# Per-layer embedding by halves of a tile, and token tiles behind both of them

## The chip, the cores and the metric

The kernel runs on one core of a Trainium2 chip. The metric is the device time of one execution in microseconds (us). All arithmetic is float32. Weight products run in the type float32r: each operand is split into a high and a low part, and three matmuls (weights low by input high, high by high, high by low) make one product.

## The reference

256 tokens of width 1024 pass through two layers of one kind and one of another. `PLAN` in the kernel lists the ten stages: ffn, even, ffn, ple, ffn, mla, ffn, ple, hybrid, ffn. The stages that matter here are:

```python
def rms_norm(x, g):
    y = x * lax.rsqrt(jnp.mean(x * x, axis=-1, keepdims=True) + EPS)
    return y * g

def swiglu(h, w_gate, w_up, w_down):
    return (jax.nn.silu(h @ w_gate) * (h @ w_up)) @ w_down

def per_layer_embedding(h, p_i, w_gate, w_proj, post_norm):
    return rms_norm(jax.nn.sigmoid(h @ w_gate) * (p_i @ w_proj), post_norm)

x = x + per_layer_embedding(rms_norm(x, g[3]), p[i], ple_w_gate[i], ple_w_proj[i], g[4])
# after the first one: x = x + 0.5 * swiglu(rms_norm(x, g[0]), ...)
# after the second one, the hybrid layer:
h = rmsnorm(x, norm_mix)
u = h @ w_in          # split into q, k, v, z, xbc (896 wide), dt_raw, p_in
y = concatenate([moba_attention(q, k, v), ssd_mixer(conv(xbc), z, dt_raw), pool_mixer(p_in)])
x = x + y @ w_out
```

`ple_w_gate` is 1024 x 1024, `ple_w_proj` 256 x 1024.

## The kernel before

**Weights.** Every weight is streamed in slots of 128 x 2048 floats (1 MB). Three raw slots form a ring (`raw`), filled by SyncE's DMAs in the order of use; `load_slot` waits until the low half of the slot three places earlier has been made (`split_ready`). ScalarE copies a raw slot into its high half (`wh`, `split_high`, L211), once the matmuls that used that place have run (`weights_used`); VectorE makes the low half (`wl`, `split_low`, L222); TensorE waits for it in `take_slot`. Slots are numbered through the program; `act_ahead.through(n)` and `dve_ahead.through(n)` issue all splits up to slot n at that place of the engine's instruction stream. So each engine's program order fixes where its splits stand among the rest.

**Columns.** The input of a product is x turned: TensorE transposes x in 128 x 128 blocks into PSUM, ScalarE scales them with the norm's gain into `hth` (high), VectorE makes `htl` (low). `turn_x`, `turn_act` and `turn_dve` do this for both token tiles (tt = 0, 1) of a pair of feature blocks k. `turn_tile`, `tile_act` and `tile_dve` (L375, L381, L388) do it for four blocks of one token tile. The row factor of the norm is applied after the product; it is the power of a mean of squares, made by GpSimd (`norm_pool`, L428 and L429).

**PLE** (`ple_pe`, `ple_act`, `ple_dve`, `ple_pool`). With n its first slot: n is the proj weight, n+1 to n+4 are the gate weight, and the next stage begins with n+5 and n+6. TensorE multiplies proj into PSUM banks 0 to 3 and then the gate into banks 4 to 7; the last two gate slots are taken tile by tile. Then, a tile at a time: sigmoid of 1024 columns (L853, ScalarE), product with the proj result (L889, VectorE), squares (L858, ScalarE) and times the gain (L894, VectorE), power (L879, GpSimd), and two additions of 512 columns into x (L901, VectorE). Each addition releases transposes of TensorE (`x_ready`).

**Behind it.** The FFN (`first_by_tiles`) takes its first two slots tile by tile: four feature blocks of tile 0 with slot n+5, four with n+6, and tile 1's transposes stand behind the sixth. The hybrid instead waits for all of x: 44 transposes of the identity fill the time (L837), sixteen transposes of x follow, and `columns_product` multiplies slots n+5 and n+6 with the weights stationary and 256 tokens moving. VectorE takes the result of these two slots (`xa`, L2338, 1024 columns) times the row factor, and later that of the next two (`xb`).

Of the kernel before, what the change touches and what calls it, by code (L numbers as in the profile page):

```python
# [31 lines left out]
def build_block(nc, io, out):  # L32
# [4 lines left out]
    P = 128  # L37
# [39 lines left out]
    with ExitStack() as stack:  # L77
# [5 lines left out]

        raw = sb("raw", [P, RING, SLOT])
# [33 lines left out]
        lb = sb("lb", [P, 3, 4])  # L118
        arena = sb("arena", [P, 20552])
# [28 lines left out]
        cols_low = sem("cols_low")  # L148
        silu_ready = sem("silu_ready")
# [45 lines left out]

        def first_part(t, n, j):

            return t[:, n, j * SLOT // 2:(j + 1) * SLOT // 2]

        def split_high(act, n):  # L200
# [8 lines left out]
            if n >= RING:  # L209
                act.wait_ge(weights_used, n - RING + 1)  # L210
            nc.scalar.activation(wh[:, n % RING, 0:width[n]], raw[:, n % RING, 0:width[n]], ACT.Copy)\  # L211
              .then_inc(high_ready, 1)

        def split_low(dve, n):
            if n < 2:
                for j, (ready, done) in enumerate(((first_high, first_low), (high_ready, split_ready))):
# [5 lines left out]
            nc.vector.tensor_tensor(wl[:, n % RING, 0:width[n]], raw[:, n % RING, 0:width[n]],  # L222
                                    wh[:, n % RING, 0:width[n]].bitcast(f32), ALU.subtract)\
# [146 lines left out]

        def turn_tile(pe, s, tt, u):

            pe.wait_ge(x_ready, 4 * (s - 1) + 2 * tt + u + 1)
            for k in range(4 * u, 4 * u + 4):
                m = nc.tensor.transpose(ps[:, 4 + 2 * tt + u, (k % 4) * P:(k % 4 + 1) * P], x[:, tt, k * P:(k + 1) * P], ident[:, :])  # L375
            m.then_inc(turned, 1)

        def tile_act(act, s, tt, u, gain):
            act.wait_ge(turned, bank_base[s][0] + 2 * tt + u + 1)
            for k in range(4 * u, 4 * u + 4):  # L380
                m = nc.scalar.activation(hth[:, k, tt * P:(tt + 1) * P], ps[:, 4 + 2 * tt + u, (k % 4) * P:(k % 4 + 1) * P], ACT.Copy,  # L381
                                         scale=cols[:, gain + k:gain + k + 1])
            m.then_inc(cols_high, 1)

        def tile_dve(dve, s, tt, u, gain):
            dve.wait_ge(cols_high, bank_base[s][0] + 2 * tt + u + 1)
            for k in range(4 * u, 4 * u + 4):
                m = nc.vector.scalar_tensor_tensor(out=htl[:, k, tt * P:(tt + 1) * P], in0=ps[:, 4 + 2 * tt + u, (k % 4) * P:(k % 4 + 1) * P],  # L388
                                                   scalar=cols[:, gain + k:gain + k + 1], in1=hth[:, k, tt * P:(tt + 1) * P].bitcast(f32),
                                                   op0=ALU.mult, op1=ALU.subtract)  # L390
            m.then_inc(cols_low, 1)

# [123 lines left out]
        def ffn_pe(pe, n, s, f):  # L516
# [51 lines left out]
            def first_by_tiles(pe):  # L568

                turn_tile(pe, s, 0, 0)  # L570
                turn_tile(pe, s, 0, 1)
                for tt in range(TT):
                    for u in range(2):
                        take_slot(pe, n + u)
                        turned_by(pe, s, 0, 2 * tt + u + 1)
                        r = (n + u) % RING
                        for kk in range(4):
                            k, at = 4 * u + kk, kk * 2 * HC
                            m = product(bank(tt), hth[:, k, tt * P:(tt + 1) * P], htl[:, k, tt * P:(tt + 1) * P],
                                        wh[:, r, at:at + 2 * HC], wl[:, r, at:at + 2 * HC], k == 0, k == KT - 1)  # L580
# [167 lines left out]
        def after_ple(s):  # L748
            return s > 0 and PLAN[s - 1:s + 1] == ["ple", "ffn"]
# [14 lines left out]
        ple_gate = Steps(sem("ple_act"), ["sigmoid0", "squares0", "sigmoid1", "squares1"], 2)  # L764
        ple_vector = Steps(sem("ple_dve"), ["product0", "gained0", "product1", "gained1"], 2)
# [6 lines left out]
        ple_ms = arena[:, 4096:4096 + TT]  # L772
# [19 lines left out]
        def ple_pe(pe, s, l):  # L792
# [31 lines left out]
            for tt in range(TT):  # L824
                for j in (2, 3):
                    take_slot(pe, n + 1 + j)
                    for kk in range(2):
                        for half in range(2):
# [1901 lines left out]
```

## Time and profile before

| | us |
|---|---|
| median of 3 runs (1378.53 to 1378.92) | 1378.87 |
| the profiled execution | 1378.48 |
| its span in the trace | 1376.7 |
| TensorE busy in the span | 1341.6 |
| VectorE busy | 796.8 |
| ScalarE busy | 645.7 |
| GpSimd busy | 82.2 |

The mean granted clock of TensorE was 0.996 of full. Matmuls are pipelined: a matmul of 512 columns stands with 0.39 us in the trace, while the next starts 0.227 us after it.

### The profile page before, as it was taken

Reading aid. Unit: us, or ns where it says so; the run is one execution under the profiler, and the core shown is the slowest. Engines: PE = TensorE matmul, PEld = TensorE weight load, DVE = VectorE, ACT = ScalarE, POOL = GpSimd, SP = SyncE. Lnnn points to the kernel's source line nnn. Section 1 sums busy time; section 2 is a strip of 40 time slices with the busy share of each in tenths; the row PEclk is TensorE's granted clock in tenths of the full one; section 3 lists DMA queues with packets and bytes.
Section 4 is the critical chain, followed back from the end, with each engine's and each line's share of the span. In section 5 each row is a group of like instructions: output and inputs, shape, how many; then the busy total and the mean of one; then the engine's idle time right before and its main releaser. Section 6 shows DMA issues by size and latency. Waiting matters only on the chain.

```text
span 1376.7 us, 17712 instructions
## 1 busy us (share of the span) xinstructions
PE 1341.6 (97%) x6710; PEld 1114.1 (81%) x6710; DVE 796.8 (58%) x873; ACT 645.7 (47%) x742; POOL 82.2 (6%) x181
## 2 busy tenths in 40 slices
PE   8999999999999999999999999999999998999998
PEld 7888889877888887788888877888887986788886
DVE  5555459746545545654556876544556887555444
ACT  5444457324444445544444856444445655444442
POOL 2000003100000001200000300000001200000000
PEclk9999999999999999999999999999999999999999
DMA  8655555414655554455553514655543452565551
GB/s 256 218 190 183 183 168 184 153 62 150 219 190 194 186 183 153 155 190 191 192 188 113 193 61 160 201 185 191 191 164 138 156 184 63 175 204 183 183 191 54
DMA packets 159326, 233.32 MB, mean 169 GB/s; under 512 B 7608, under 2 KB 126542, under 8 KB 159278
## 3 DMA queue, kind: packets, MB, share of 16 engines
q1 hardware_dynamic: 156560, 229.17, 50.5%
q10 hardware_dynamic: 2238, 2.70, 0.6%
q0 software_dynamic: 480, 0.80, 0.4%
q8 instruction: 32, 0.52, 0.2%
q14 instruction: 16, 0.13, 0.0%
HBM read 231.58 MB, written 1.05 MB: 169 GB/s over the span
## 4 chain that ended last, share of the span: by engine, by line
PE 92%; DVE 4%; ACT 2%; issue 1%; DMA 0%; POOL 0%; ACTq 0%; DVEq 0%; POOLq 0%
PE ps L250 27%; PE ps L252 26%; PE ps L251 26%; PE ps L545 2%; DVE wl L222 1%; PE ps L1012 1%; PE ps L266 1%; PE ps L334 1%; PE ps L268 1%; PE ps L267 1%; DVE htl L367 1%; PE ps L1526 1%; PE ps L1525 1%; ACT wh L211 1%; ACT hth L354 0%
## 5 line engine op out<-in xcount | busy, mean ns | idle before, releaser
L250 PE MATMUL ps<-wl,hth 128*128 128x512 f32 (+2 forms) x1280 | 504.6, 394 | 14.5 <-DVE htl L367 5.8
L252 PE MATMUL ps<-wh,htl 128*128 128x512 f32 (+2 forms) x1280 | 494.7, 386 | 0.0
L251 PE MATMUL ps<-wh,hth 128*128 128x512 f32 (+2 forms) x1280 | 493.9, 386 | 0.0
L714 DVE TENSOR_TENSOR wl<-raw,wh 128x2048 fp32r<-128x2048 f32 x120 | 275.1, 2292 | 204.9 <-ACT wh L663 204.9
L250 PEld LDWEIGHTS ps<-wl,hth 128*128 128x128 f32 x1280 | 240.5, 188 | 65.0 <-issue 15.2
L663 ACT ACTIVATE wh<-raw 128x2048 fp32r<-128x2048 f32 x120 | 229.7, 1914 | 123.6 <-PE ps L252 123.6
L252 PEld LDWEIGHTS ps<-wh,htl 128*128 128x128 f32 x1280 | 240.3, 188 | 49.3
L251 PEld LDWEIGHTS ps<-wh,hth 128*128 128x128 f32 x1280 | 240.8, 188 | 44.6
L222 DVE TENSOR_TENSOR wl<-raw,wh 128x2048 fp32r<-128x2048 f32 (+3 forms) x98 | 217.1, 2223 | 79.5 <-ACT wh L211 79.3
L211 ACT ACTIVATE wh<-raw 128x2048 fp32r<-128x2048 f32 (+3 forms) x98 | 181.0, 1853 | 65.7 <-PE ps L252 45.5
L250 PE MATMUL ps<-wl,prod_h 128*128 128x512 f32 x400 | 156.1, 390 | 0.0
L252 PE MATMUL ps<-wh,prod_l 128*128 128x512 f32 x400 | 155.8, 390 | 0.0
L251 PE MATMUL ps<-wh,prod_h 128*128 128x512 f32 x400 | 155.6, 389 | 0.0
L650 ACT ACTIVATE silu_g<-ps,rstd 128x256 f32<-128x256 f32 x110 | 46.3, 472 | 173.2 <-PE ps L252 173.2
L655 ACT ACTIVATE prod_h<-ps 128x512 fp32r<-128x512 f32 x50 | 29.9, 599 | 156.3 <-PE ps L545 156.3
L700 DVE SCALAR_TENSOR_TENSOR prod<-ps,rstd,silu_g 128x256 f32<-128x256 f32 x110 | 48.2, 479 | 83.7 <-ACT silu_g L650 83.7
L252 PEld LDWEIGHTS ps<-wh,prod_l 128*128 128x128 f32 x400 | 75.1, 188 | 15.6
L251 PEld LDWEIGHTS ps<-wh,prod_h 128*128 128x128 f32 x400 | 75.1, 188 | 15.4
L250 PEld LDWEIGHTS ps<-wl,prod_h 128*128 128x128 f32 x400 | 75.1, 188 | 15.4
L707 DVE TENSOR_TENSOR prod_l<-ps,prod_h 128x512 fp32r<-128x512 f32 x50 | 34.6, 692 | 71.7 <-ACT prod_h L655 71.7
L428 POOL TENSOR_SCALAR mean_sq<-mean_sq 128x1 f32<-128x1 f32 x20 | 8.4, 420 | 864.6 <-ACT xn L415 860.9
L354 ACT ACTIVATE hth<-ps,cols 128x256 fp32r<-128x256 f32 x77 | 30.3, 478 | 49.6 <-PE ps L334 44.4
(377 smaller groups left out, 990.7 us busy)
## 6 DMA issues: line engine op xcount, KB each, us to landing
raw<-in_ffn_w_down SPq DMA_DIRECT2D x88, 512.0 KB, 4.0
raw<-in_ffn_w_gate SPq DMA_DIRECT2D x86, 512.0 KB, 4.0
raw<-in_ffn_w_up SPq DMA_DIRECT2D x86, 512.0 KB, 4.9
raw<-in_w_gate_up SPq DMA_DIRECT2D x44, 512.0 KB, 4.7
raw<-in_even_w_in SPq DMA_DIRECT2D x24, 512.0 KB, 4.6
raw<-in_w_down SPq DMA_DIRECT2D x22, 512.0 KB, 3.6
raw<-in_ple_w_gate SPq DMA_DIRECT2D x16, 512.0 KB, 4.1
raw<-in_w_in SPq DMA_DIRECT2D x16, 512.0 KB, 4.4
```

Source lines behind the costliest of these rows:

```text
L211: nc.scalar.activation(wh[:, n % RING, 0:width[n]], raw[:, n % RING, 0:width[n]], ACT.Copy)\
L222: nc.vector.tensor_tensor(wl[:, n % RING, 0:width[n]], raw[:, n % RING, 0:width[n]], wh[:, n % RING, 0:width[n]].bitcast(f32), ALU.subtract)\
L250: nc.tensor.matmul(o, xh, b, start=first, stop=False)
L251: nc.tensor.matmul(o, xh, a, start=False, stop=False)
L252: return nc.tensor.matmul(o, xl, a, start=False, stop=last)
L354: m = nc.scalar.activation(dst[:, k, :], ps[:, banks[b], o:o + T], ACT.Copy, scale=g)
L650: nc.scalar.activation(silu_g[:, tt, :], ps[:, b + tt, 0:HC], ACT.Silu, scale=rstd[:, tt:tt + 1]).then_inc(silu_ready, 1)
L655: nc.scalar.activation(to[:, :, :], bank(b).rearrange("p (k t) -> p k t", k=2), ACT.Copy)\
L663: nc.scalar.activation(wh[:, r, :], raw[:, r, :], ACT.Copy).then_inc(high_ready, 1)
L700: m = nc.vector.scalar_tensor_tensor(out=prod[:, tt, :], in0=ps[:, b + tt, HC:2 * HC], scalar=rstd[:, tt:tt + 1], in1=silu_g[:, tt, :], op ...
L707: nc.vector.tensor_tensor(to[:, :, :], bank(b).rearrange("p (k t) -> p k t", k=2), high[:, :, :].bitcast(f32), ALU.subtract).then_inc(prod ...
L714: nc.vector.tensor_tensor(wl[:, r, :], raw[:, r, :], wh[:, r, :].bitcast(f32), ALU.subtract)\
```

## The change

- Two spare pairs of weight halves, `spare_h` and `spare_l`, lie over a part of the arena that PLE and the start of the next stage don't use. The two slots behind each PLE (n+5, n+6) are split into them; ScalarE's split of these waits for the raw data and for no matmul. ScalarE and VectorE issue the splits through n+6 ahead of the sigmoids.
- VectorE splits slot n+1 between the first and the second pair of column banks.
- Sigmoid, product, squares and gain are done in halves of 512 columns; GpSimd adds the two sums of squares.
- The last gate slot's pieces are sorted by half, and TensorE's first four transposes of x (tile 0) stand ahead of the last gate piece of tile 1. Tile 1's transposes stand behind the whole of tile 0's products.
- The columns of a tile are handed on first as a pair of blocks (`pair_high`, `pair_low`), then the rest of the four; they lie in other PSUM banks.
- The hybrid, too, begins by tiles: its first two slots are multiplied for 128 tokens at a time, with one PSUM bank for each tile and slot, so VectorE adds the slots' results up. The 44 filler transposes are gone.

```diff
+        SPARE = 10240
+        with ExitStack() as lower:
+            lower.enter_context(nc.sbuf_tensor("below_spare", [P, SPARE], f32))
+            spare_h = lower.enter_context(nc.sbuf_tensor("spare_h", [P, 2, SLOT], f32r))
+            spare_l = lower.enter_context(nc.sbuf_tensor("spare_l", [P, 2, SLOT], f32r))
         arena = sb("arena", [P, 20552])
+        spare = {base[s] + u: u for s in range(1, len(PLAN)) if PLAN[s - 1] == "ple" for u in range(2)}
...
-            if n >= RING:
+            if n >= RING and n not in spare:
                 act.wait_ge(weights_used, n - RING + 1)
-            nc.scalar.activation(wh[:, n % RING, 0:width[n]], raw[:, n % RING, 0:width[n]], ACT.Copy)\
+            nc.scalar.activation(high_of(n)[:, 0:width[n]], raw[:, n % RING, 0:width[n]], ACT.Copy)\
...
+        def tile_bank(tt, u, i):
+            return 4 + 2 * tt + i if u == 0 else (1, 5)[tt]
+        def tile_by(pe, s, tt, k):
+            if k == 0:
+                pe.wait_ge(pair_low, TT * ples[s - 1] + tt + 1)
+            if k in (2, 4):
+                turned_by(pe, s, 0, 2 * tt + k // 4 + 1)
...
             def first_by_tiles(pe):
-                turn_tile(pe, s, 0, 0)
-                turn_tile(pe, s, 0, 1)
                 for tt in range(TT):
                     for u in range(2):
                         take_slot(pe, n + u)
-                        turned_by(pe, s, 0, 2 * tt + u + 1)
                         for kk in range(4):
                             k, at = 4 * u + kk, kk * 2 * HC
+                            tile_by(pe, s, tt, k)
...
-                            if tt == 0 and k == 5:
-                                turn_tile(pe, s, 1, 0)
-                                turn_tile(pe, s, 1, 1)
+                    if tt == 0:
+                        turn_tile(pe, s, 1, 0)
+                        turn_tile(pe, s, 1, 1)
...
         def ple_pe(pe, s, l):
+                    pieces = [(kk, half) for kk in range(2) for half in range(2)]
+                    if j == 3:
+                        pieces.sort(key=lambda v: v[1])
+                    for i, (kk, half) in enumerate(pieces):
+                        if tt == 1 and j == 3 and i == 3:
+                            turn_tile(pe, s + 1, 0, 0)
+                        m = gate_piece(j, kk, half, tt)
+                        if j == 3 and (i == 1 or (i == 3 and tt == 0)):
+                            m.then_inc(tile_ready, 1)
...
-            for _ in range(0 if after_ple(s + 1) else 44):
-                nc.tensor.transpose(ps[:, 4, 0:P], ident[:, :], ident[:, :])
+            turn_tile(pe, s + 1, 0, 1)
         def ple_act(act, s, l):
-            act_ahead.through(act, n + 5)
+            act_ahead.through(act, n + 6)
...
+            sigmoid(0, 0)
+            sigmoid(0, 1)
+            squares(0, 0)
+            squares(0, 1)
+            sigmoid(1, 0)
+            tile_act(act, s + 1, 0, 0, gain_behind(s + 1))
+            sigmoid(1, 1)
+            tile_act(act, s + 1, 0, 1, gain_behind(s + 1))
+            squares(1, 0)
+            squares(1, 1)
+            act.wait_ge(ple_vector.sem, ple_vector.after("gained11", l))
+            nc.scalar.activation(xn[:, 0, :], x[:, 0, :], ACT.Square, scale=1 / math.sqrt(D),
+                                 accum_out=mean_sq[:, 0:1]).then_inc(sq_ready, 1)
+            act_ahead.through(act, n + 7)
         def ple_dve(dve, s, l):
-            turn_dve(dve, s, 1, KT, GAINS + (5 * l + 3) * KT, PLE_BANKS)
-            dve_ahead.through(dve, n + 5)
+            turn_dve(dve, s, 1, KT, GAINS + (5 * l + 3) * KT, PLE_BANKS, part=(0, 2))
+            dve_ahead.through(dve, n + 1)
+            turn_dve(dve, s, 1, KT, GAINS + (5 * l + 3) * KT, PLE_BANKS, part=(2, 4))
+            dve_ahead.through(dve, n + 6)
...
+            gated(0, 0)
+            gated(0, 1)
             gain(0)
             add(0)
+            gated(1, 0)
+            tile_dve(dve, s + 1, 0, 0, gain_behind(s + 1))
+            gated(1, 1)
+            tile_dve(dve, s + 1, 0, 1, gain_behind(s + 1))
             gain(1)
             add(1)
...
+        PART_BANK = ((0, 4), (2, 3))
         def hybrid_pe(pe, s):
-            for b in range(4):
-                turn_x(pe, s, b, b)
-            columns_product(pe, n, [bank(4 + j, T) for j in range(4)], 512, first_of=s)
+            for tt in range(TT):
+                for u in range(2):
+                    take_slot(pe, n + u)
+                    for j in range(4):
+                        for kk in range(4):
+                            k = 4 * u + kk
+                            if j == 0:
+                                tile_by(pe, s, tt, k)
+                            o, c = ps[:, PART_BANK[tt][u], j * P:(j + 1) * P], kk * 512 + j * P
+                            a, b = high_of(n + u)[:, c:c + P], low_of(n + u)[:, c:c + P]
+                            nc.tensor.matmul(o, b, hth[:, k, tt * P:(tt + 1) * P], start=kk == 0, stop=False)
+                            nc.tensor.matmul(o, a, hth[:, k, tt * P:(tt + 1) * P], start=False, stop=False)
+                            m = nc.tensor.matmul(o, a, htl[:, k, tt * P:(tt + 1) * P], start=False, stop=kk == 3)
...
+                if tt == 0:
+                    turn_tile(pe, s, 1, 0)
+                    turn_tile(pe, s, 1, 1)
...
         def hybrid_dve(dve, s):
-            HY_DVE.done(nc.vector.tensor_tensor(h_x[:, 0:4, PADC:PADC + T], ps[:, 4:8, 0:T], repeated(r_row[:, :], 1, 4), ALU.mult), "xa")
+            parts = [h_x[:, 0:4, PADC + tt * P:PADC + (tt + 1) * P] for tt in range(TT)]
+            for tt in range(TT):
+                a, b = (bank(PART_BANK[tt][u]).rearrange("p (j c) -> p j c", j=4) for u in range(2))
+                r = repeated(r_row[:, tt * P:(tt + 1) * P], 1, 4)
+                nc.vector.tensor_tensor(parts[tt], a, r, ALU.mult)
+                m = nc.vector.tensor_tensor(h_c[:, 0:4, tt * P:(tt + 1) * P], b, r, ALU.mult)
+            dve_link(dve, m)
+            for tt in range(TT):
+                m = nc.vector.tensor_tensor(parts[tt], parts[tt], h_c[:, 0:4, tt * P:(tt + 1) * P], ALU.add)
+            HY_DVE.done(m, "xa")
```

`norm_tiles_act` and `tile_dve` take the place of `norm_act` and `norm_dve` at the hybrid's start, and the p product's results lie in banks 2 and 3 in place of 4 and 5.

## Rows read from the trace of the kernel before

**Rows 1.** The page: busy time by engine, and the chain that ended last by engine.

```profile
PE 1341.6 (97%) x6710; PEld 1114.1 (81%) x6710; DVE 796.8 (58%) x873; ACT 645.7 (47%) x742; POOL 82.2 (6%) x181
...
PE 92%; DVE 4%; ACT 2%; issue 1%; DMA 0%; POOL 0%; ACTq 0%; DVEq 0%; POOLq 0%
```

**Rows 2.** Timeline of PE (start, duration, instruction, idle before): first gate matmul.

```profile
526.06 0.47 PE L250 MATMUL ps<-wl,hth 128*128 128x512 f32 x1 [1.71 <-DVE wl L222]
```

**Rows 3.** Timeline of DVE, start of the first PLE.

```profile
518.44 1.66 DVE L367 SCALAR_TENSOR_TENSOR htl<-ps,cols,hth 128x256 fp32r<-128x256 f32 x4
522.06 1.66 DVE L367 SCALAR_TENSOR_TENSOR htl<-ps,cols,hth 128x256 fp32r<-128x256 f32 x4 [1.96 <-ACT hth L354]
523.64 4.48 DVE L222 TENSOR_TENSOR wl<-raw,wh 128x2048 fp32r<-128x2048 f32 x2
```

**Rows 4.** Timeline of POOL, the two powers of the norm.

```profile
526.09 2.46 POOL L429 TENSOR_TENSOR rstd<-mean_sq,minus_half 128x1 f32<-128x1 f32 x1
...
528.93 0.57 POOL L429 TENSOR_TENSOR rstd<-mean_sq,minus_half 128x1 f32<-128x1 f32 x1
```

**Rows 5.** Timeline of ACT, first PLE.

```profile
522.63 1.94 ACT L211 ACTIVATE wh<-raw 128x2048 fp32r<-128x2048 f32 x1
...
529.53 1.92 ACT L211 ACTIVATE wh<-raw 128x2048 fp32r<-128x2048 f32 x1 [2.89 <-POOL rstd L429]
...
539.26 1.28 ACT L853 ACT_TABLE_LOAD   x1
542.71 1.12 ACT L853 ACTIVATE xn<-ps,rstd 128x1024 f32<-128x1024 f32 x1 [2.16 <-PE ps L252]
...
548.97 2.18 ACT L381 ACTIVATE hth<-ps,cols 128x128 fp32r<-128x128 f32 x8 [0.83 <-PE ps L375]
```

**Rows 6.** Line L179, 534.1 to 535 us: slot n+6's two loads until landed.

```profile
DMA to landing us min/median/max: 4.0/4.5/5.0
```

**Rows 7.** Timeline of DVE, end of the first PLE.

```profile
547.41 1.42 DVE L901 SCALAR_TENSOR_TENSOR x_rows<-arena,x_rows 128x512 f32<-128x512 f32 x2 [1.00 <-POOL arena L879]
550.15 2.16 DVE L388 SCALAR_TENSOR_TENSOR htl<-ps,cols,hth 128x128 fp32r<-128x128 f32 x8 [1.33 <-ACT hth L381]
```

**Rows 8.** Timeline of PE, first PLE to the FFN's third slot.

```profile
548.30 1.23 PE L375 MATMUL ps<-ident,x_rows 128*128 128x128 f32 x8 [0.19 <-DVE x_rows L901]
551.42 0.47 PE L250 MATMUL ps<-wl,hth 128*128 128x512 f32 x1 [1.88 <-DVE htl L388]
...
561.18 0.48 PE L250 MATMUL ps<-wl,hth 128*128 128x512 f32 x1 [0.44 <-DVE htl L388]
...
566.72 0.39 PE L250 MATMUL ps<-wl,hth 128*128 128x512 f32 x1
```

**Rows 9.** Timeline of PE, second PLE and the hybrid's start.

```profile
1060.49 4.96 PE L837 MATMUL ps<-ident 128*128 128x128 f32 x44
...
1068.64 0.36 PE L266 MATMUL ps<-hth,wl 128*128 128x256 f32 x1 [0.62 <-DVE htl L367]
...
1080.21 0.61 PE L458 MATMUL ps<-silu_g,ones 128*128 128x128 f32 x4
...
1100.60 0.60 PE L2024 MATMUL ps<-ident,arena 128*128 128x128 f32 x4
```

**Rows 10.** Timeline of PE elsewhere: narrow matmuls in the even and the mla stage.

```profile
272.69 2.26 PE L1048 MATMUL ps<-arena 64*128 64x128 f32 x24
...
754.94 0.27 PE L250 MATMUL ps<-wl,hth 128*128 128x192 f32 x1
...
757.17 0.27 PE L252 MATMUL ps<-wh,htl 128*128 128x192 f32 x1
```

**Rows 11.** Timeline of DVE, start of the hybrid.

```profile
1081.32 1.22 DVE L2338 TENSOR_TENSOR arena<-ps,r_row 128x1024 f32<-128x1024 f32 x1
...
1089.42 1.24 DVE L222 TENSOR_TENSOR wl<-raw,wh 128x1048 fp32r<-128x1048 f32 x1
...
1098.35 2.28 DVE L222 TENSOR_TENSOR wl<-raw,wh 128x2048 fp32r<-128x2048 f32 x1
```

More of the change, by code:

```diff
@@ L856, in squares @@
-            def squares(tt):
-                act.wait_ge(ple_vector.sem, ple_vector.after(f"product{tt}", l))
-                ple_gate.done(nc.scalar.activation(ple_sq[:, tt, :], xn[:, tt, :], ACT.Square, scale=1 / math.sqrt(D),
-                                                   accum_out=ple_ms[:, tt:tt + 1]), f"squares{tt}", l)
-            sigmoid(0)
-            squares(0)
-            act_ahead.through(act, n + 6)
-            if after_ple(s + 1):
-                for u in range(2):
-                    tile_act(act, s + 1, 0, u, FFN_GAIN[fs[s + 1]])
@@ L867, in ple_act @@
-            sigmoid(1)
-            squares(1)
-            if after_ple(s + 1):
-                nc.scalar.activation(xn[:, 0, :], x[:, 0, :], ACT.Square, scale=1 / math.sqrt(D),
-                                     accum_out=mean_sq[:, 0:1]).then_inc(sq_ready, 1)
-                act_ahead.through(act, n + 7)
+                ple_gate.done(nc.scalar.activation(part(tt, half), bank(4 + 2 * tt + half), ACT.Sigmoid, scale=rstd[:, tt:tt + 1]),
+                              f"sigmoid{tt}{half}", l)
@@ new lines, in squares @@
+            def squares(tt, half):
+                act.wait_ge(ple_vector.sem, ple_vector.after(f"product{tt}{half}", l))
+                at = 2 * tt + half
+                ple_gate.done(nc.scalar.activation(ple_sq[:, tt, half * 512:(half + 1) * 512], part(tt, half), ACT.Square,
+                                                   scale=1 / math.sqrt(D), accum_out=ple_ms[:, at:at + 1]), f"squares{tt}{half}", l)
+            sigmoid(0, 0)
+            sigmoid(0, 1)
+            squares(0, 0)
+            squares(0, 1)
@@ L876, in ple_pool @@
             for tt in range(TT):
-                pool.wait_ge(ple_gate.sem, ple_gate.after(f"squares{tt}", l))
-                pool_link(pool, nc.gpsimd.tensor_scalar(ple_ms[:, tt:tt + 1], ple_ms[:, tt:tt + 1], EPS, None, ALU.add))
-                ple_rstd.done(nc.gpsimd.tensor_tensor(ple_rs[:, tt:tt + 1], ple_ms[:, tt:tt + 1], minus_half[:, 0:1],
-                                                      ALU.pow), f"rstd{tt}", l)
+                a, b = (ple_ms[:, 2 * tt + half:2 * tt + half + 1] for half in range(2))
@@ L882, in ple_dve @@
+                pool.wait_ge(ple_gate.sem, ple_gate.after(f"squares{tt}0", l))
+                pool_link(pool, nc.gpsimd.tensor_scalar(a, a, EPS, None, ALU.add))
+                pool.wait_ge(ple_gate.sem, ple_gate.after(f"squares{tt}1", l))
+                pool_link(pool, nc.gpsimd.tensor_tensor(a, a, b, ALU.add))
+                ple_rstd.done(nc.gpsimd.tensor_tensor(ple_rs[:, tt:tt + 1], a, minus_half[:, 0:1], ALU.pow), f"rstd{tt}", l)
         def ple_dve(dve, s, l):
             n = base[s]
-            turn_dve(dve, s, 1, KT, GAINS + (5 * l + 3) * KT, PLE_BANKS)
@@ L2313, in hybrid_dve @@
             n = base[s]
-            norm_dve(dve, s, MIX2)
+            for u in range(2):
+                tile_dve(dve, s, 1, u, MIX2)
+            dve_ahead.through(dve, n + 1)
             rms_diagonals(dve, s, 1)
             dve_ahead.before(dve, n + 1)
-            rms_row(dve, 1, 3)
+            rms_row(dve, 1, 1)
             def convolve(ks):
```

99 lines of the change are left out of this document (55 added, 44 removed).

## The prediction

> **What bounds the kernel.** First the busy line of the page and the chain's shares [rows 1]: TensorE is busy 1341.6 of 1376.7 us and carries 92% of the chain, nearly all of it in weight matmuls, so only what idles TensorE or lengthens its own work moves the time. 35 us of idle exist in all. Then the timelines, engine by engine, around the two per-layer embeddings ("PLE"), the only stages edited: the first ends at 548 us (an FFN follows), the second at 1060 us (the hybrid follows). The trace shows three places.
> - The first gate matmul waits 1.71 us for a low half of a weight slot [rows 2]. VectorE had idled 1.96 us just before, waiting for ScalarE's columns, with that slot's high half long there [rows 3].
> - Between PLE and FFN TensorE goes 548.30 transposes, 551.42 first product, 561.18 second tile, 566.72 next slot [rows 8]. The gate's 96 matmuls from 526.06 at 0.228 end it at 547.95. From there to 566.72 are 18.8 us, of which 48 matmuls (24 take 561.18 to 566.72, 5.5 us) fill 10.9 and 16 transposes 1.8: 6 are idle.
> - Between PLE and hybrid it is 1060.49 to 1068.64, 8.15 us without a product, of which 4.96 is filler transposes [rows 9].
>
> The working runs against the profiled execution, 1378.48 us (span 1376.7 plus 1.8 around it), which is 0.39 below the median 1378.87; I add the difference of the sum to the median.
>
> **Part 1, first gate slot.** VectorE will do columns 0 and 1 (ends 520.1), then the split at once (2.2 of the 4.48 for two: ends 522.3), then columns 2 and 3 (1.66: ends 523.9) [rows 3]. TensorE has its proj product until 524.2, so the gate starts at 524.2 in place of 526.06: 1.87 us earlier at both PLEs. This only counts if what follows is earlier too, so I follow it.
>
> **Part 2, who feeds the sigmoid.** ScalarE must now split slots up to n+6 ahead of the sigmoid (before: n+5); the spare halves take away the waits for used slots at n+5 and n+6, not the wait for the raw data. Raw slot n+6 is loaded when VectorE has split n+3, which waits for ScalarE's split at 529.53, and that for the GpSimd power [rows 5]. The power took 2.46 us against 0.57 for the next, ending 0.43 after VectorE's two splits did (528.12) [rows 3, 4]. VectorE's second split will run 524.6 (ScalarE's high half, 522.63+1.94) to 526.9, so the power ends 527.3, ScalarE starts n+3 at 528.3: 1.2 earlier. Then VectorE's n+3 ends 532.5, the load's second half issues at about 533.0 and lands 5.0 later [rows 6], at 538.0; ScalarE splits n+6 until 539.95 and loads its table (1.28 [rows 5]) until 541.2. TensorE has the first half of tile 0 at 539.2, so ScalarE, not TensorE, is late here, by 2.0: the sigmoid starts 541.25 against 542.71, 1.46 earlier and not more.
>
> Behind VectorE's own split of n+6 (until 542.25) stand the product, the gains and the adds of tile 0. Halves of 512 columns cost 0.65 to 0.7 each (two adds of 512 take 1.42 [rows 7], 1024-wide operations 1.12 to 1.22 [rows 5, 11]): products 542.2 to 543.45, squares behind them by halves, the last with its read at 544.25. GpSimd gains one add and stands behind VectorE's gains until 544.7; its add and power (0.57 [rows 4]) end 545.5. x's first half is written 546.25, against 548.1 (547.41 + 0.71 [rows 7]).
>
> **Part 3, PLE to FFN.** TensorE reaches the transposes of tile 0, now ahead of its last gate piece, at 545.3 and waits 1.1 for x: 546.45. Last piece until 547.7, other transposes until 548.2. Two high columns come 0.67+0.65 after the transposes began (as 548.30 to 548.97 [rows 5, 8]), at 547.75; their two low ones (eight take 2.16 [rows 7]) at 548.4; the first product is at 548.5 against 551.42 [rows 8]. Waiting for a pair instead of four saves 0.5 of this. The four stall-free pieces and the next (slot n+6 is split by then: its 1.26 us wait is gone) end tile 0 at 554.05. Meanwhile: second columns high 550.05, squares of tile 1 until 551.45, gains until 552.5, power 553.2, x 554.05; tile 1's transposes 554.15 to 555.3. ScalarE now waits for the last gain, squares x (1.1) from 552.55 and splits n+7 (1.9) until 555.5, and only then makes tile 1's columns: TensorE idles about 1.6 and starts tile 1 at 556.9, done 5.5 later at 562.4. Against 566.72: **−4.3 us**. The next slots (n+7 low at 561.3) are in time.
>
> **Part 4, PLE to hybrid.** The second gate ends at 1060.49 [rows 9], the first at 547.95: the same steps 512.54 later put the first product at 1061.0 against 1068.64. But its 96 matmuls of 256 columns, 1068.64 to 1080.21, 0.1205 each [rows 9], become 192 of 128 columns, each with its own 128-column weight load. The trace has no float32r pair that narrow. The nearest row: 192 columns, same operands, 754.94 to 757.17, 20 steps of 0.1115 [rows 10]; columns fell from 256 to 192 there and the step by only 7%, and the fillers, 128 columns wide, take 4.96−0.27 over 43 steps, 0.109 [rows 9]. So the weight load is the floor, and I take 0.1115. Low end: L1048, weights of 64 rows, 24 in 2.26, (2.26−0.28)/23 = 0.086 [rows 10]; high end 0.1205, as now. That is 21.4 us for 11.57. Sequence: 1061.0; tile 0 takes 10.7, and 0.1 for its second pair: 1071.8; eight transposes 0.9; tile 1's first columns are ready 2.05 after these began, 1073.9 (1.2 idle); 10.7 more: 1084.6 against 1080.21: **+4.4 us**. The filler's end is worth nothing by itself: its place was idle.
>
> The Trainium skill, "TensorE: Matmul & The Clock Gate", section "Back-to-back issue gap", gives 81 ns for a sustained load-and-matmul pair at 128 columns; by it the 192 would cost 15.6 us, 5.8 less, and this part −1.4. The same page, section "LDWEIGHTS", makes a load of 128 columns 107 ns, which the 192-column row agrees with; I go by the row.
>
> **Part 5, xa on VectorE.** The 1024-wide product 1.22 [rows 11] becomes four of 512 from PSUM (2.5), a chained wait and two adds of 512 (1.3): 3.8, so 2.6 more, at a place where its timeline then shows no idle over 0.3 until past 1100. Behind it stand the splits n'+4 to n'+7 and the convolutions (n' the hybrid's first slot). Slot n'+5 is low at 1090.66 (1089.42+1.24) and TensorE wants it at 1092.2 (1100.60 [rows 9] less 24 at 0.227 and 24 at 0.12): 1.05 late now. Slot n'+7 is low at 1100.63 (1098.35+2.28 [rows 11]) and wanted 1101.0 (1100.60+0.44 [rows 9]): late by 2.6 less 0.3 of idle taken up and less this margin of 0.4. The delays overlap: **+1.9 us** in all. The ends are nothing (all covered) and 3.0 (no slack, and a wait more). The p product moves from banks 4, 5 to 2, 3 at no cost: it waits for xa as before.
>
> **Sum.** −4.3 + 4.4 + 1.9 = +2.0: 1378.48 becomes 1380.5, and the median 1380.9. Within 0.2% (2.76 us, about what a measurement of this kernel can tell from no change).
>
> **Rivals.**
> - *Narrow pairs go faster than the 192-column row* (0.086, the low end): 192 × 0.0255 = 4.9 less, −2.9: 1376.0, faster. For it: L1048 shows such a step, where the stationary block has 64 rows. Against: here it has 128 rows, and both full-height rows sit at 0.109 and 0.1115. Chance 0.11. The 81 ns of the Trainium skill's page above would be this rival with another size.
> - *The power is not released early* (other side). If GpSimd's power still ends at 528.5, because other VectorE work stands in its way or because it is simply slow the first time, the load of n+6 lands at 539.2, the sigmoid starts at 542.45, and both PLEs end 1.2 later: +4.4, 1383.3, slower. It decides from 0.4 us of delay at each (the sum then passes +2.76). For it: 2.46 against 0.57. Against: its end fits the end of the splits to 0.43. A stall of n+6 through queued loads acts at the same place. Chance 0.27.
> - *The xa detour is covered*, VectorE's lateness taken up by slack: 1379.0, no change. Against: two slots with margins under 1.6. Chance 0.13.
> - *ScalarE is not late for the sigmoid*: if n+6 lands 1 us sooner (its load no longer shares the queue), each PLE gains up to 1.0, with the xa stall as forecast: 0.0, 1378.9. Chance 0.09.
> - *Forecast*: 0.40.
>
> **Numbers.** The range reaches from the narrow-pair case (1376.0) to the late power with a little more xa stall: 1375.8 to 1384.0. The forecast alone spans 1379 to 1382.5. Slower by over 0.2%: the late power 0.25 and 0.08 of the forecast's upper side. Faster: 0.11, 0.04 where the third and fourth meet, and 0.03 of the forecast. The same: the rest, 0.49.
>
> **What would show it.** Right: first gate matmul without idle, 1.9 earlier; the power at about 1.2; a sigmoid starting right behind ScalarE's split and table load, not on TensorE; PLE end to the FFN's third slot about 2.4 shorter apart from the gate's shift; 192 matmuls of 128 columns over 21 us; TensorE idle for VectorE's wl in the first slots after xa, about 2 in all. Wrong: a step near 0.08 for the narrow pairs, a power of 2.4 again, no wl wait in the hybrid, or a granted clock below full around the removed filler (idle stretches of 1.7 to 1.9 us before left it full; I expect none longer).

## The result and the profile after

| kernel | median us | range, runs | ratio to before, 95% interval |
|---|---|---|---|
| before | 1378.6 | 1377.31 to 1382.41, 17 | |
| changed | 1381.19 | 1379.34 to 1383.14, 17 | 1.0018 [1.0011, 1.0026] |

The forecast was 1380.9 us, the same as before within 0.2%; measured is 1381.19, slower by 0.18%, a difference small but clear of noise (the interval leaves out 1). The profiled execution took 1382.67 us with a span of 1380.9, against 1376.7.

First the page of the changed kernel, its busy line and the chain by engine:

```profile
PE 1349.9 (98%) x6762; PEld 1122.3 (81%) x6762; DVE 800.5 (58%) x894; ACT 648.4 (47%) x762; POOL 78.6 (6%) x185
...
PE 89%; DVE 5%; ACT 3%; DMA 1%; issue 1%; POOL 1%; ACTq 0%; SPq 0%; DVEq 0%; POOLq 0%
```

TensorE is busy 8.3 us longer than before [rows 1] while the span grew by 4.2: idle time was traded for work, and the trade lost. Some 2.4 us of the 8.3 are a stretch at the lower clock, shown below. Its share of the chain fell from 92 to 89%, while those of VectorE, ScalarE, DMA and GpSimd rose by one point each.

To see where, take TensorE's timeline at fixed points and measure each from the x transposes that open the PLE (516.94 in the kernel before, 516.18 after; the 0.76 arise before anything that was changed: an FFN's product at 330.65 in the kernel before stands at 329.88 in the changed one). The changed kernel, first PLE (start, duration, instruction, idle before):

```profile
516.18 1.03 PE L350 MATMUL ps<-ident,x_rows 128*128 128x128 f32 x8
...
523.44 0.39 PE L266 MATMUL ps<-wl,hth 128*128 128x512 f32 x1
...
545.83 0.65 PE L400 MATMUL ps<-ident,x_rows 128*128 128x128 f32 x4 [1.15 <-DVE x_rows L957]
...
547.93 0.47 PE L266 MATMUL ps<-spare_l,hth 128*128 128x512 f32 x1 [0.32 <-DVE htl L419]
...
553.56 1.03 PE L400 MATMUL ps<-ident,x_rows 128*128 128x128 f32 x8
555.92 0.47 PE L266 MATMUL ps<-spare_l,hth 128*128 128x512 f32 x1 [1.33 <-DVE htl L419]
561.51 0.39 PE L266 MATMUL ps<-wl,hth 128*128 128x512 f32 x1
```

These answer to [rows 2, 8]. The gate starts without idle, 7.26 us behind the first transposes where it was 9.12. The idle of 1.88 before the first product is now 1.15 before the transposes and 0.32 behind them. The FFN's third slot begins 45.33 behind the first transposes where it was 49.78 (566.72): 4.45 less.

The same engine, second PLE and hybrid, answering to [rows 9]:

```profile
1024.26 1.03 PE L350 MATMUL ps<-ident,x_rows 128*128 128x128 f32 x8
...
1055.93 0.30 PE L2073 MATMUL ps<-hth,spare_l 128*128 128x128 f32 x1 [0.32 <-DVE htl L419]
...
1066.67 1.06 PE L400 MATMUL ps<-ident,x_rows 128*128 128x128 f32 x8
1068.75 0.30 PE L2073 MATMUL ps<-hth,spare_l 128*128 128x128 f32 x1 [1.02 <-DVE htl L419]
1079.49 0.66 PE L498 MATMUL ps<-silu_g,ones 128*128 128x128 f32 x4
...
1092.63 0.39 PE L266 MATMUL ps<-wl,hth 128*128 128x262 f32 x1 [0.94 <-DVE wl L238]
1101.33 0.60 PE L2096 MATMUL ps<-ident,arena 128*128 128x128 f32 x4
1102.26 0.50 PE L266 MATMUL ps<-wl,hth 128*128 128x512 f32 x1 [0.33 <-DVE wl L238]
1107.85 0.82 PE L2108 MATMUL ps<-ident,arena 128*128 128x128 f32 x6
```

Each tile's 96 narrow matmuls take 10.74 us (1055.93 to 1066.67), 0.112 each. The head of the hybrid ends at 1079.49, 55.23 behind this PLE's first transposes (1024.26); before it was 50.74 (1029.47 to 1080.21): 4.49 more. Then two waits for VectorE's low halves, and the transposes of L2108 (L2036 before, at 1106.51, 77.04 behind) stand 83.59 behind: 2.06 more.

VectorE behind the head, the first and the last of its operations for xa, answering to the first of [rows 11]:

```profile
1080.65 0.69 DVE L2416 TENSOR_TENSOR arena<-ps,r_row 128x512 f32<-128x512 f32 x1
...
1083.17 1.29 DVE L2420 TENSOR_TENSOR arena<-arena 128x512 f32<-128x512 f32 x2
```

From 1080.65 to 1084.46 (1083.17 + 1.29) it is busy with six operations where one of 1.22 stood.

In all −4.45 + 4.49 + 2.06 = +2.1 us. The profiled executions differ by 4.2 in span. −0.76 is the start; the other 2.9 are in a place that no edit touches, TensorE's idle time before the last FFN. Its matmuls there in the kernel before, then in the changed kernel, and below them the changed kernel's windows of 5 us (engines' busy us in the order PE, PEld, DVE, ACT, POOL; then the granted clock):

```profile
1183.87 0.47 PE L250 MATMUL ps<-wl,hth 128*128 128x512 f32 x1 [2.76 <-DVE htl L367]
...
1186.71 1.03 PE L334 MATMUL ps<-ident,x_rows 128*128 128x128 f32 x8
```

```profile
1185.28 0.77 PE L266 MATMUL ps<-wl,hth 128*128 128x512 f32 x1 [2.76 <-DVE htl L383]
...
1190.53 1.50 PE L350 MATMUL ps<-ident,x_rows 128*128 128x128 f32 x8
```

```profile
1180.00:1185.00 5.00, 2.52 (x16) 1.96 (x14) 2.27 (x5) 1.57 (x4) 0.00 (x0) 0.96 0.18 66
1185.00:1190.00 5.00, 4.72 (x11) 3.83 (x12) 3.12 (x4) 0.00 (x0) 0.00 (x0) 0.50 0.23 75
1190.00:1195.00 5.00, 5.00 (x24) 4.16 (x24) 1.66 (x4) 3.37 (x7) 0.59 (x2) 0.85 0.45 174
```

The same idle of 2.76 us stands in both kernels. In this execution the granted clock behind it was 0.50, TensorE's lower level of 1.2 GHz, and twelve matmuls took 5.25 us; in the profiled execution of the kernel before they took 2.84 (1183.87 to 1186.71), at a granted clock of 1.00. So these 2.4 us, and the few tenths behind them, are no part of the change until shown to be.

### The profile page after: what moved, and what is told of

Its sections match the earlier page's. It is cut to its first block, busy times and chain, and to the rows that moved or that the text cites. A ratio compares the mean times of both kernels' runs of the same rounds, so it can differ in the third digit from the quotient of the medians.

```text
span 1380.9 us, 17862 instructions
## 1 busy us (share of the span) xinstructions
PE 1349.9 (98%) x6762; PEld 1122.3 (81%) x6762; DVE 800.5 (58%) x894; ACT 648.4 (47%) x762; POOL 78.6 (6%) x185
## 4 chain that ended last, share of the span: by engine, by line
PE 89%; DVE 5%; ACT 3%; DMA 1%; issue 1%; POOL 1%; ACTq 0%; SPq 0%; DVEq 0%; POOLq 0%
PE ps L266 26%; PE ps L268 25%; PE ps L267 25%; PE ps L585 2%; DVE wl L238 2%; PE ps L1067 1%; PE ps L350 1%; ACT wh L227 1%; PE ps L1581 1%; DVE arena L2404 1%; PE ps L282 1%; PE ps L283 1%; PE ps L284 1%; PE ps L2073 1%; PE ps L2075 1%
## 5 line engine op out<-in xcount | busy, mean ns | idle before, releaser
L266 PE MATMUL ps<-wl,hth 128*128 128x512 f32 (+2 forms) x1264 | 499.1, 395 | 8.8 <-DVE htl L383 5.8
L268 PE MATMUL ps<-wh,htl 128*128 128x512 f32 (+2 forms) x1264 | 489.4, 387 | 0.0
L267 PE MATMUL ps<-wh,hth 128*128 128x512 f32 (+2 forms) x1264 | 488.6, 387 | 0.0
L238 DVE TENSOR_TENSOR wl<-raw,wh 128x2048 fp32r<-128x2048 f32 (+3 forms) x94 | 207.9, 2219 | 75.0 <-ACT wh L227 74.9
L227 ACT ACTIVATE wh<-raw 128x2048 fp32r<-128x2048 f32 (+3 forms) x94 | 173.1, 1851 | 58.6 <-PE ps L268 37.4
L370 ACT ACTIVATE hth<-ps,cols 128x256 fp32r<-128x256 f32 x69 | 27.3, 477 | 50.0 <-PE ps L350 44.7
```

Of the source, the lines that this page charges most:

```text
L227: nc.scalar.activation(high_of(n)[:, 0:width[n]], raw[:, n % RING, 0:width[n]], ACT.Copy)\
L238: nc.vector.tensor_tensor(low_of(n)[:, 0:width[n]], raw[:, n % RING, 0:width[n]], high_of(n)[:, 0:width[n]].bitcast(f32), ALU.subtract)\
L266: nc.tensor.matmul(o, xh, b, start=first, stop=False)
L267: nc.tensor.matmul(o, xh, a, start=False, stop=False)
L268: return nc.tensor.matmul(o, xl, a, start=False, stop=last)
```

## The experiments

All times are compared with runs of the kernel before on the same chip. "Behind T2" is the distance from the second PLE's first x transposes; "PLE 1 stage" the distance from the first PLE's first transposes to T2 (512.53 before, 508.08 changed). A half-clock stretch outside a distance doesn't enter it, so the distances compare where the whole times don't.

**Wide hybrid head.** The changed kernel, with tiles only where an FFN follows:

```
+        def tiles_behind(s):
+            return PLAN[s + 1] == "ffn"
...
-            turn_tile(pe, s + 1, 0, 1)
+            if tiles_behind(s): turn_tile(pe, s + 1, 0, 1)
+            else: (wait for sigmoid00; 44 filler transposes)
...
+            for b in range(4):
+                turn_x(pe, s, b, b)
+            columns_product(pe, n, [bank(4 + j, T) for j in range(4)], 512, first_of=s)
```

> The changed kernel, with the hybrid's head as it was before (256-column matmuls over both tiles, 44 fillers behind the second PLE, one wide xa); the tiles, the spare slots and the sooner split stay at both PLEs, the token tiles only behind the first. Theory (all of the loss sits in the 128-column matmuls and in the xa that they leave to VectorE): PLE 1 to the FFN's third slot stays 4.45 us shorter, the second gate ends 1.9 us sooner than in the kernel before, nothing waits for xa, so the p turn and what follows stand some 6 us earlier than before: about 1372 us, 0.995 of the kernel before. Rival A (the hybrid's own beginning is set by something that both forms share, as the norm or the splits of the slots behind): at most 2 us of the 6.5 us between the two forms come back, about 1376.5 to 1379 us. Rival B (the second PLE by halves gives the wide head nothing, since its x comes whole): 1374 us, only the first PLE's share.

Measured: 1371.24 us (1370.9 to 1372.78, 5 runs), ratio 0.9947 [0.9934, 0.9961]. TensorE's timeline of this kernel:

```profile
1025.72 1.03 PE L350 MATMUL ps<-ident,x_rows 128*128 128x128 f32 x8
...
1054.74 4.96 PE L889 MATMUL ps<-ident 128*128 128x128 f32 x44
1059.54 1.91 PE L350 MATMUL ps<-ident,x_rows 128*128 128x128 f32 x16
1062.08 0.36 PE L282 MATMUL ps<-hth,spare_l 128*128 128x256 f32 x1 [0.62 <-DVE htl L383]
...
1099.33 0.82 PE L2107 MATMUL ps<-ident,arena 128*128 128x128 f32 x6
```

The first product is 36.36 behind T2, 2.81 less than before (39.17), and L2107 73.61 behind, 3.43 less than before and 9.98 less than in the changed kernel. With 4.34 less in the PLE 1 stage that makes 7.8; measured are 7.4. Both rivals fall. The narrow head alone takes 10 us away from a change that otherwise gains 7: more than the 4.4 + 1.9 that I had priced, because those were against the kernel before, whose wide head begins later. Of the 3.43, 0.6 arise behind the first product, and the traces say where: the same 96 matmuls of 256 columns take 10.97 us here (1062.08 to 1073.05), 0.114 each, against 11.57 before. Why they go faster in this kernel is open.

**xa from one bank.** Two operations in place of six; the first slot's part is left out of the sum:

```
-                nc.vector.tensor_tensor(parts[tt], a, r, ALU.mult)
-                m = nc.vector.tensor_tensor(h_c[:, 0:4, ...], b, r, ALU.mult)
-            dve_link(dve, m)
-            ... parts[tt] + h_c
+                m = nc.vector.tensor_tensor(parts[tt], b, r, ALU.mult)
```

> The changed kernel, where xa takes only the second slot's banks (two 512-wide operations instead of four operations over 1024 columns twice; the part of the first slot is left out of the sum, so half of these products is missing from the result). Theory: VectorE is 2.6 us earlier at the splits of the sixth and eighth slots, the 0.94 us wait before the 262-column matmuls and the later one before the p turn's successors go, and everything behind the hybrid's head is 2.0 us earlier than in the changed kernel. Rival (the splits are late for another reason, as the weights' landing or ScalarE's high half): the waits stay, the p turn within 0.3 us of the changed kernel's.

Measured: 1379.86 us, one run. TensorE's timeline:

```profile
1069.16 0.30 PE L2073 MATMUL ps<-hth,spare_l 128*128 128x128 f32 x1 [1.02 <-DVE htl L419]
...
1106.24 0.82 PE L2108 MATMUL ps<-ident,arena 128*128 128x128 f32 x6
```

Between the second tile and L2108 there is no wait left. T2 was 1024.81, so L2108 is 81.43 behind it: 2.16 less than changed. What remains against the kernel before, 4.39, is the narrow head by itself. The theory holds for both terms. It rests on these distances: the single run's time lies 1.3 us under the changed kernel's median and inside its range.

**Which operand sets a narrow step.** In the hybrid's first two slots tile 0 moves 64 tokens past 128-column weights, and tile 1 moves 128 tokens past 64-column weights:

```
+                            w, q = (P // 2, P) if tt == 0 else (P, P // 2)
+                            o, a, b = o[0:q, 0:w], a[:, 0:q], b[:, 0:q]
```

> The changed kernel; in the hybrid's first two slots tile 0 moves only 64 tokens past 128-column weights, tile 1 moves 128 tokens past 64-column weights (half of these products is left out). Theory (the load of a 128-column float32r weight is the floor of a narrow matmul): tile 0 stays near 0.111 us per matmul though it moves half as much, tile 1 falls well under 0.09. Rival (the moving columns, or a fixed gap per matmul, are the floor): tile 0 falls to 0.06 to 0.085, tile 1 stays at 0.111.

The timeline of tile 0, then of tile 1:

```profile
1059.58 0.28 PE L2077 MATMUL ps<-htl,spare_h 128*128 128x64 f32 x1
...
1060.47 0.28 PE L2076 MATMUL ps<-hth,spare_h 128*128 128x64 f32 x1
...
1061.64 0.40 PE L2075 MATMUL ps<-hth,spare_l 128*128 128x64 f32 x1
```

```profile
1080.68 0.22 PE L2077 MATMUL ps<-htl,spare_h 128*64 128x128 f32 x1
...
1081.75 0.22 PE L2077 MATMUL ps<-htl,spare_h 128*64 128x128 f32 x1
```

Eight steps at full clock take 0.89 us (1059.58 to 1060.47): 0.111 each with half the moving tokens. With half-wide weights eighteen steps take 1.07: 0.059 each. So the floor of the matmuls with 128-column weights is the weight load, and halving the tokens under it changes nothing. With 64-column weights it is open which side is the floor: 128 moving columns would take 0.057 at the pace of the 512-column matmuls (0.227 each), an estimate that is as near 0.059 as half a load is. Within tile 0 the granted clock fell to its lower level (from 1061 on the records read 0.40 in place of 0.28, and a step takes 0.213 in place of 0.111), so tile 0 took 16.8 us in place of 10.7, and this run 1383.41.

**The splits into the spare slot behind the first tile.** At both PLEs:

```
-            act_ahead.through(act, n + 6)
+            act_ahead.through(act, n + 5)
 (squares of tile 0)
+            act_ahead.through(act, n + 6)
-            dve_ahead.through(dve, n + 6)
+            dve_ahead.through(dve, n + 5)
 (first low parts of tile 0)
+            dve_ahead.through(dve, n + 6)
```

> The changed kernel, with the two splits into the spare slot (ScalarE's and VectorE's of the seventh) moved behind the first tile's squares and behind the first half's low parts, at both PLEs. Theory: ScalarE reaches the first sigmoid as soon as TensorE's sums are there (near 538.6 in the changed kernel's time instead of 540.88) and the FFN's first product comes 0.8 to 1.0 us earlier; it is kept through tile 1 only if the split is still ready for the third slot. Rival (VectorE's chain, product, square and low parts, sets the first product): sigmoid earlier, product unchanged within 0.3 us. A second rival: the gain is given back whole at the second tile or the third slot, where the late split ends last.

Measured: 1381.56 us, one run. ScalarE's and TensorE's timelines:

```profile
539.62 0.69 ACT L900 ACTIVATE xn<-ps,rstd 128x512 f32<-128x512 f32 x1 [3.92 <-PE ps L268]
```

```profile
547.60 0.47 PE L266 MATMUL ps<-spare_l,hth 128*128 128x512 f32 x1 [0.32 <-DVE htl L419]
551.96 0.47 PE L266 MATMUL ps<-spare_l,hth 128*128 128x512 f32 x1 [1.35 <-DVE htl L419]
557.29 0.47 PE L266 MATMUL ps<-spare_l,hth 128*128 128x512 f32 x1 [1.43 <-DVE htl L419]
```

The sigmoid now waits for TensorE, and the first product is 30.39 behind the first transposes (517.21) where it was 31.75: 1.36 earlier. The theory had put that at 0.8 to 1.0. Behind it VectorE's split (547.89, 2.28 long) holds up the second pair of low parts, TensorE waits 1.35 in the middle of tile 0, and the stage is 0.38 longer than changed: the second rival, for the FFN. Behind the second PLE, where tile 0 is 10.7 us long instead of 5.5, the gain stays: L2110 82.33 behind T2, 1.26 less than changed. So ScalarE was late for the sigmoid, as the prediction's part 2 has it. Where an FFN follows, moving the split behind the sigmoid gains nothing, because VectorE's split is then late in turn.

**The sooner split alone.** The kernel before with one edit:

```
-            turn_dve(dve, s, 1, KT, GAINS + ..., PLE_BANKS)
+            turn_dve(dve, s, 1, KT, GAINS + ..., PLE_BANKS, part=(0, 2))
+            dve_ahead.through(dve, n + 1)
+            turn_dve(dve, s, 1, KT, GAINS + ..., PLE_BANKS, part=(2, 4))
```

> The kernel before with the first gate slot's split moved up alone (behind the low parts of the first two banks of x, at both PLEs), no halves, no spare slots, no token tiles. Theory: the gate's first matmul comes 1.87 us earlier at both PLEs; behind the second it passes down to the hybrid, behind the first to the FFN, less what the splits behind it hold back: 1.5 to 3.7 us under the kernel before. Rival (the GpSimd power or ScalarE's split of a later slot ends last): the gate starts earlier and what follows stands where it did, 0 to 1 us.

Measured: 1374.81 us (1373.68 to 1377.87, 9 runs), ratio 0.9974 [0.9964, 0.9984]. TensorE's timeline:

```profile
524.92 0.39 PE L250 MATMUL ps<-wl,hth 128*128 128x512 f32 x1
...
565.47 0.39 PE L250 MATMUL ps<-wl,hth 128*128 128x512 f32 x1
...
1065.36 0.35 PE L266 MATMUL ps<-hth,wl 128*128 128x256 f32 x1 [0.63 <-DVE htl L367]
```

The gate starts 7.25 behind the first transposes (517.67) and 1.87 us earlier than before; the FFN's third slot begins 47.80 behind them, 1.98 less; the PLE 1 stage is 510.52, 2.01 less; the hybrid's first product is 37.17 behind T2 (1028.19), 2.00 less. Nothing holds any of it back, and the gain of 3.9 us lies a little above the 1.5 to 3.7 expected. Of the 7.4 us that the wide head gains, three lines of code are 3.9.

**The idle time before the last FFN.** Five kernels fill it with 22 transposes of the identity: the changed, the wide-headed and the kernel before at all three FFNs that don't follow a PLE, then two of them at the last FFN only.

```
                 turn_x(pe, s, 1, FFN_BANKS[1])
+                if s > 0:          (later: and PLAN[s - 1] == "hybrid")
+                    for _ in range(22):
+                        nc.tensor.transpose(ps[:, 1, 0:P], ident[:, :], ident[:, :])
```

> The changed kernel with 22 transposes of the identity in TensorE's idle time behind the x transposes of each FFN that doesn't follow a PLE (three of them; 2.8 us idle before the last one). Theory (the 2.7 us that the profiled run of the changed kernel loses at half clock behind the last hybrid comes of that idle stretch, by chance of where it falls): no half-clock stretch there in any run, the times move together near 1379.5 us, the span's mean granted clock 0.998 in each; the fillers cost under 0.3 us each. Rival (the drop has to do with something else, as the load before it): the mean clock still varies between 0.995 and 0.998 and the spread of 1379.3 to 1383.1 stays.

> The wide-headed hybrid with the tiles behind the first PLE alone, and the 22 fillers at the three FFNs. Theory: its time is that of the wide head, some 6.5 us under the kernel before (near 1372 us), with less spread, 0 to 1.5 us under the same kernel without fillers. Rival: fillers delay the transposes of the second half of x and cost 0.5 to 1 us at each of the three FFNs.

> The kernel before with the same 22 fillers at the three FFNs and nothing else. Theory (the drop at that idle is by chance and hits the kernel before too, in some of its runs): median 0 to 1.2 us under the kernel before, spread smaller. Rival (only the changed kernel drops there): no difference, or slower by up to 1 us by the fillers themselves.

> The wide-headed hybrid with the tiles behind the first PLE alone, and 22 transposes of the identity in TensorE's 2.8 us idle stretch before the last FFN only (in the kernel with three such places the other two were idle for only 1.5 us and cost 0.7 to 0.9 us each). Theory: no half-clock stretch there, no cost at the other places: 1370.3 to 1371 us, all runs near together; 0.995 or less of the kernel before. Rival (the drop has another cause): 1371.2 us and the spread of 1370.9 to 1372.8 as without fillers.

> The changed kernel with the same 22 transposes before the last FFN only. Theory (two things move the changed kernel's time from run to run: a half-clock stretch at that idle time, 0 to 2.7 us, and a rarer one among the 128-column matmuls, 7.7 us): the runs gather at 1379.3 to 1380.4 us, with at most one in five near 1388. Rival: the spread of 1379.3 to 1383.1 stays.

| kernel | places | median us (range, runs) | ratio to before, 95% |
|---|---|---|---|
| changed | 3 | 1381.98 (1381.51 to 1389.77, 10) | 1.0029 [1.0017, 1.004] |
| wide head | 3 | 1372.37 (1371.61 to 1372.98, 5) | 0.9951 [0.9938, 0.9964] |
| before | 3 | 1379.46 (1378.94 to 1380.13, 11) | 1.0005 [0.9996, 1.0014] |
| wide head | last | 1370.66 (1369.68 to 1371.44, 5) | 0.9941 [0.9928, 0.9955] |
| changed | last | 1380.39 (1379.69 to 1381.94, 11) | 1.0012 [1.0003, 1.0021] |

Seven profiled kernels without the fillers have this idle time, 2.76 or 2.77 us long. In five of them (changed, wide head, one-bank xa, late splits, sooner split) the granted clock fell behind it, and the twelve matmuls there took 4.38 to 5.25 us; in the kernel before and in the one of the operand experiment it did not, and they took 2.84 and 2.85. In the five with fillers it never fell there. The clearest pair is the changed kernel's windows above and the second of the same windows with the fillers at the last FFN:

```profile
1185.00:1190.00 5.00, 4.64 (x29) 3.86 (x28) 3.86 (x5) 1.19 (x4) 0.00 (x0) 1.00 0.27 98
```

So the drop goes with that idle time; its size differs from run to run, and the kernel of the operand experiment shows that a changed kernel can be without it. That the kernel before has it in other runs isn't shown, since it was profiled only once without fillers. The fillers were mis-sized at first. In the kernel before, the idle time at the other two FFNs is 1.50 us and not 2.8, as this row of its timeline has it at one of them:

```profile
330.65 0.47 PE L250 MATMUL ps<-wl,hth 128*128 128x512 f32 x1 [1.50 <-DVE htl L367]
```

and 22 transposes overrun it, here in the same kernel with them:

```profile
329.24 2.56 PE L553 MATMUL ps<-ident 128*128 128x128 f32 x22
331.56 0.48 PE L250 MATMUL ps<-wl,hth 128*128 128x512 f32 x1
```

The product came 2.53 us behind the x transposes (328.12) and comes 3.20 behind them (328.36): some 0.7 lost at each of the two. So the three kernels with three filled places came out above the times expected of them, by 0.7 to 1.1 us over the same kernels without fillers. For the kernel before that is 0.74 (1379.46 against 1378.72), and 1.34 were lost; an estimate from these is that some 0.6 came back at the last FFN there too. At the last FFN alone the fillers are free (the product comes 3.80 us behind the x transposes in the wide head with them and without), and the wide head with them is the fastest version, 8.2 us under the kernel before. Against 1371.24 without them the 0.6 us lie inside the spread of five runs; against the changed kernel the median went from 1381.19 to 1380.39, with a spread of 2.3 in place of 3.8, wider than the 1379.3 to 1380.4 expected.

One thing no theory had: two of the ten runs of the changed kernel with three filled places took 1389.8 us, and the profiled one was of these. Its windows over the narrow matmuls:

```profile
1060.00:1070.00 10.00, 9.92 (x89) 9.68 (x88) 3.23 (x7) 3.68 (x8) 2.82 (x5) 1.00 0.01 2
1070.00:1080.00 10.00, 9.07 (x54) 9.10 (x55) 4.40 (x11) 5.17 (x12) 5.61 (x44) 0.68 0.21 62
1080.00:1090.00 10.00, 10.00 (x49) 10.00 (x49) 1.76 (x1) 1.26 (x2) 0.00 (x0) 0.50 0.31 105
```

The clock fell at 1073.6, 2.7 us into tile 1, whose first product had waited 1.02 us as in the changed kernel; TensorE's records are busy almost throughout. And the p turn's transposes came 84.7 behind T2 in place of 77.1: 7.7 us. None of 17 runs of the changed kernel and none of 11 with the last place filled is as long, so it is rare; the run with 64 moving tokens had it too.

## Why the prediction was right

- *Part 1, the gate 1.87 earlier.* 1.86 measured in the changed kernel, 1.87 in the kernel with this edit alone, at both PLEs.
- *Part 2, the power released early.* The timelines of VectorE and GpSimd in the changed kernel, and below them a row of GpSimd's in the kernel before, which stands ahead of [rows 4]:

```profile
523.84 2.29 DVE L238 TENSOR_TENSOR wl<-raw,wh 128x2048 fp32r<-128x2048 f32 x1 [0.72 <-ACT wh L227]
524.93 1.28 POOL L468 TENSOR_SCALAR mean_sq<-mean_sq 128x1 f32<-128x1 f32 x1 [186.95 <-ACT xn L455]
526.30 0.56 POOL L469 TENSOR_TENSOR rstd<-mean_sq,minus_half 128x1 f32<-128x1 f32 x1
```

```profile
525.68 0.32 POOL L428 TENSOR_SCALAR mean_sq<-mean_sq 128x1 f32<-128x1 f32 x1 [186.95 <-ACT xn L415]
```

  The long instruction is no longer the power but the one ahead of it, and it ends at 526.21, as VectorE's split does (523.84 + 2.29 = 526.13). Before, the power took 2.46 and ended 0.43 behind VectorE's two splits [rows 3, 4]. There the operation ahead of it took only 0.32 and ended at 526.00, about as the first of the two splits did (half of their 4.48 from 523.64 is 525.88); the power began under the second. So in both kernels what stretches is the GpSimd operation that starts while a split of VectorE runs, to about that split's end, whichever of the two it is. Nor is the power slow the first time: here it took 0.56. That rival (0.27) is out. ScalarE's split of n+3 began at 527.85; counted from the earlier start 527.5 were forecast.
- *Part 2, ScalarE late for the sigmoid.* Its timeline, answering to [rows 5]:

```profile
537.65 1.92 ACT L227 ACTIVATE spare_h<-raw 128x2048 fp32r<-128x2048 f32 x1 [4.18 <-DMA raw<-in_ffn_w_up]
539.59 1.28 ACT L900 ACT_TABLE_LOAD   x1
540.88 1.27 ACT L900 ACTIVATE xn<-ps,rstd 128x512 f32<-128x512 f32 x2
```

  The sigmoid is 1.07 earlier net, where 1.46 was forecast, behind the landing, the split and the table load in the order predicted. The experiment with late splits shows that ScalarE was what it waited for (1.36 us on the first product), so the rival at 0.09 is out. Its price, up to 1.0 per PLE, was not tested: no run has the load landing sooner, and that would bring VectorE's split forward too, which the late splits don't.
- *Part 3, −4.3.* −4.45. The wait before tile 1 was put at 1.6 and is 1.33.
- *Part 4, +4.4.* +4.49, and 4.39 in the run without xa's detour. 192 steps at 0.112; the experiment on the operands shows why the 192-column row was the right one to take: the step is the weight load, 0.111 with 64 moving tokens and 0.059 with 64 weight columns. L1048's 0.086 [rows 10] has weights of 64 rows, not of fewer columns; the narrow pairs with 128 rows don't go at that pace, and why those of 64 do is open. The Trainium skill, "TensorE: Matmul & The Clock Gate", section "Back-to-back issue gap", has 81 ns for a pair at 128 columns; here it is 112, and the measurement decides. The formula of its section "LDWEIGHTS" gives 107 ns for a load of 128 columns (an estimate by that page), which is near the 0.111 and 0.112 us of these runs.
- *Part 5, +1.9.* +2.06, and 2.16 by the run that takes the detour away. The rival that it is covered is out.
- *The sum.* +2.1 where +2.0 stood. The medians differ by 2.6, their interval is 1.5 to 3.6. With the same fillers at three places in both kernels the medians differ by 2.5 (1381.98 against 1379.46). The condition named as a sign of error, a granted clock below full around the removed filler, was absent in the changed kernel's profile, but it did come in two variants of it, among the narrow matmuls (the operand experiment, and the changed kernel with three places filled, where two of ten runs were some 7 us longer than the rest and the profiled one of them shows it). In the changed kernel the clock fell at the idle time before the last FFN, 2.76 us long in the kernel before already, a place that the prediction doesn't price. That the median came within 0.3 us of the forecast is partly chance: from the base of 1378.6 measured with it, the sum gives 1380.6.

What the prediction did not ask is what each part is worth by itself. It priced the hybrid's token tiles against the old kernel and found the sum near nothing; the answer that matters to whoever tunes on is that two of the parts gain 7.4 us and the third takes 10 away.

## What to carry to other kernels

Cutting the moving side of a matmul from 256 to 128 columns doubles the number of weight loads, and the load is the floor: begin by token tiles only where the moving side stays wide (here the FFN, whose weights move in 512 columns past the tokens), and keep the wide form where the weights are the stationary side. Price each part of a change by itself and against the best mix of the others, not only the sum against the old kernel. Before filling TensorE's idle time, measure that idle time at each place where the loop or helper will issue the fillers.

## What the hardware showed that was not expected

- The granted clock fell to 0.50 behind an idle time of 2.76 us in five of seven profiled kernels without fillers and in none of five with; idle times of 1.5 to 1.9 us never had it in these profiles.
- It fell, too, inside a dense row of matmuls with 128-column weights: once with 64 moving columns, once with 128, where engine records show 90 to 100% busy. What makes the difference between those runs and the others is open. At 0.50 a pair with 128-column weights took 0.213 us in both, in place of 0.111 and 0.112, so the weight load slows with the clock.
- A small GpSimd operation that starts while a split of VectorE runs stretches to about that split's end (1.28 us, and 2.46 before, against 0.22 and 0.57 for the same ones just after). The sooner split alone shows it again (1.29). What holds it was not tried.
- With weights of 64 columns a pair with 128 moving columns ran at 0.059 us, about half of the pair with 128-column weights.
